# Splitting 520 tokens 240/280 instead of 260/260 in the dense products of a float32r macaron decoder layer

## The reference

```python
def half_ffn(x, g_pre, wg, wu, wd, g_post):
    return x + 0.5 * rmsnorm(swiglu(rmsnorm(x, g_pre), wg, wu, wd), g_post)
...
    hp = half_ffn(yp, *ffn1)
    fq, fk, fv, logf, nq, nkv, ng = project(rmsnorm(hp, g_mix_pre[l]), w_in[l], b_fox_f[l], pos_p)
    o_fox = fox_attention(fq, fk, fv, jnp.cumsum(logf, axis=1), pos_p)
    o_nsa = nsa_attention(nq, ng, nkv[:, :, :4], nkv[:, :, 4:], 0, pos_p, *cmp_w)
    hp = hp + rmsnorm(merge_groups(o_fox, o_nsa, g_fox_out[l], g_nsa_out[l], w_out[l]), g_mix_post[l])
    yp = half_ffn(hp, *ffn2)
```

## Time and profile before

| | |
|---|---|
| median of 3 runs | 1329.59 us (1329.27 to 1329.98) |
| span of the profiled execution | 1327.7 us; the median run is 1.9 us longer |
| PE busy / weight loads busy | 95% / 85% of the span |
| DVE, ACT, POOL busy | 43%, 34%, 13% |
| mean DMA rate | 89 GB/s |
| mean granted TensorE clock | 0.981 |

### The profile page before, as it was taken

The page is one execution under the profiler, slowest core; times in us unless marked ns, Lnnn a source line. Parts: engine busy times, 40 slices in busy tenths (PEclk is TensorE's granted clock), DMA queues, the critical chain, the costliest instruction groups (busy, mean ns, idle before and its releaser), DMA issues.

```text
span 1327.7 us, 22995 instructions
## 1 busy us (share of the span) xinstructions
PE 1259.9 (95%) x9234; PEld 1121.9 (85%) x9234; DVE 569.3 (43%) x896; ACT 454.3 (34%) x767; POOL 174.6 (13%) x157
## 2 busy tenths in 40 slices
PE   8999999999998898999999988798999999999994
PEld 6999999999996895499566543596999999999993
DVE  4334333343337665456533542636433333343333
ACT  5222212222335635442533432345322221222342
POOL 0111100101114001122101100034011100001113
PEclk9999999999999999999999989899999999999997
DMA  6222233222231241011600544011122222322221
GB/s 254 96 95 95 72 96 111 80 88 83 80 123 41 74 144 48 1 64 65 211 0 0 193 117 137 32 65 64 64 95 95 79 87 95 109 79 92 80 80 65
DMA packets 46001, 117.91 MB, mean 89 GB/s; under 512 B 4154, under 2 KB 21818, under 8 KB 39874
## 3 DMA queue, kind: packets, MB, share of 16 engines
q1 hardware_dynamic: 42738, 110.95, 24.8%
q10 hardware_dynamic: 3184, 5.88, 1.2%
HBM read 110.93 MB, written 7.97 MB: 90 GB/s over the span
## 4 chain that ended last, share of the span: by engine, by line
PE 87%; DVE 5%; ACT 3%; issue 2%; DMA 1%; POOL 1%; POOLq 0%; ACTq 0%; SPq 0%; DVEq 0%
PE ps L1308 68%; PE ps L1465 5%; PE ps L1479 3%; PE ps L1436 3%; PE ps L1451 2%; DVE UT L890 1%; PE ps L1317 1%; PE ps L1599 1%; DVE XL L870 1%; POOL H L1252 1%; DVE QST L964 1%; ACT QST L674 1%; PE ps L1608 1%; DMA RAW<-in_w_gu 0%; PE ps L1401 0%
## 5 line engine op out<-in xcount | busy, mean ns | idle before, releaser
L1308 PE MATMUL ps<-XH,WH 128*128 128x260 f32 x1904 | 390.6, 286 | 20.0 <-DVE XL L870 13.7
L1308 PE MATMUL ps<-XH,WL 128*128 128x260 f32 x1904 | 384.6, 284 | 0.0
L1308 PE MATMUL ps<-XL,WH 128*128 128x260 f32 x1904 | 384.2, 283 | 0.0
L403 ACT CAST WH<-RAW 128x1024 fp32r<-128x1024 f32 (+2 forms) x183 | 174.8, 956 | 505.1 <-PE ps L1308 495.8
L1308 PEld LDWEIGHTS ps<-XH,WH 128*128 128x128 f32 x1904 | 295.7, 189 | 27.6 <-DVE XL L870 14.0
L1308 PEld LDWEIGHTS ps<-XH,WL 128*128 128x128 f32 x1904 | 294.5, 189 | 0.0
L1308 PEld LDWEIGHTS ps<-XL,WH 128*128 128x128 f32 x1904 | 294.0, 189 | 0.0
L406 DVE TENSOR_TENSOR WL<-RAW,WH 128x1024 fp32r<-128x1024 f32 (+2 forms) x183 | 203.5, 1112 | 154.8 <-ACT WH L403 153.6
L1308 PE MATMUL ps<-UL,WH 128*128 128x260 f32 x704 | 141.9, 283 | 0.0
L1308 PE MATMUL ps<-UH,WL 128*128 128x260 f32 x704 | 141.5, 282 | 0.0
L1308 PE MATMUL ps<-UH,WH 128*128 128x260 f32 x704 | 141.4, 282 | 0.0
(11 more groups left out here) (229 smaller groups left out, 1056.5 us busy)
## 6 DMA issues: line engine op xcount, KB each, us to landing
RAW<-in_w_gu SPq DMA_DIRECT2D x44, 1024.0 KB, 4.8
RAW<-in_w_down SPq DMA_DIRECT2D x16, 768.0 KB, 4.6
RAW<-in_w_in SPq DMA_DIRECT2D x11, 1024.0 KB, 4.8
RAW<-in_w_down SPq DMA_DIRECT2D x16, 640.0 KB, 4.3
KF<-in_fox_k SPq DMA_DIRECT2D x16, 256.0 KB, 4.1
VF<-in_fox_v SPq DMA_DIRECT2D x16, 256.0 KB, 5.8
RAW<-in_w_out SPq DMA_DIRECT2D x4, 1024.0 KB, 5.0
H<-in_x SPq DMA_DIRECT2D x4, 520.0 KB, 7.4
```

Source lines behind the costliest of these rows:

```text
L403: nc.scalar.copy(WH[:, par, 0:width], RAW[:, slot, j, 0:width]).then_inc(w_hi, 1)
L1308: q = nc.tensor.matmul(ps[:, 2 * slot + half, 0:HALF], w[:, par, cols], x[:, kt0 + kt, half * HALF:(half + 1) * HALF], start=first and kt ...
```

## The change

`NA = 240` tokens are taken apart from the other 280. XH and XL become the two halves of one tile XX, UH and UL of one tile UU. Of a block, WH multiplies the high and the low part of the 240 tokens in one matmul of 480 columns; the two results lie side by side in one bank and are not added there. The 280 tokens go to the other bank with WH (high part), WH (low part) and WL, and WL·high of the 240 tokens is added onto the high result. The five matmuls have 480, 280, 280, 240 and 280 columns.

Whoever takes a tile out of PSUM must now add the low result to the high one. In `ffn` ACT first copies the low result (`lo_out`); DVE scales the 280 tokens, adds, and scales the 240 tokens (`scaled`). In `project` and for the output projection DVE does the copy as well.

```diff
@@ layer_kernel
+        def sums(slot):
+            a, b = 2 * slot, 2 * slot + 1
+            return ps[:, a, 0:NA], ps[:, a, NA:2 * NA], ps[:, b, 0:TOK - NA]
@@ scalar: ffn
                 def body(st):
+                    k = st.M * 2 + IT_F[f]
+                    if st.kind == "gu":
+                        act.wait_ge(used, k + 1)
+                        lo_out(GT[:, st.par, :], 0)
                     split_behind(f, st, 0)
...
+                        act.wait_ge(used, k + 2)
+                        lo_out(UT[:, st.par, :], 1)
+                    elif st.g == 0:
+                        act.wait_ge(used, k + 2)
+                        lo_out(row(Y, st.m), st.par)
                     split_behind(f, st, 1)
@@ vector
+            def scaled(dst, slot, f, n, downs):
+                a_hi, _, b = sums(slot)
+                nc.vector.tensor_tensor(dst[:, NA:TOK], b, R1[:, NA:TOK], ALU.mult)
+                dve.wait_ge(sem("lo_out"), since("lo_out", f, n + downs))
+                nc.vector.tensor_tensor(dst[:, 0:NA], dst[:, 0:NA], a_hi, ALU.add).then_inc(sem("joined"), 1)
+                dve.wait_ge(sem("joined"), since("joined", f, n))
+                return nc.vector.tensor_tensor(dst[:, 0:NA], dst[:, 0:NA], R1[:, 0:NA], ALU.mult)
@@ vector: ffn, down tiles of the second group
-                        nc.vector.tensor_tensor(two(row(Y, st.m)), two(row(Y, st.m)), halves(st.par),
-                                                ALU.add).then_inc(sem("evac"), 2)
+                        nc.vector.tensor_tensor(y[:, 0:NA], y[:, 0:NA], a_lo, ALU.add).then_inc(sem("joined"), 1)
+                        nc.vector.tensor_tensor(y[:, NA:TOK], y[:, NA:TOK], b, ALU.add)
+                        dve.wait_ge(sem("joined"), since("joined", f, st.m + (2 * FT + 1)))
+                        nc.vector.tensor_tensor(y[:, 0:NA], y[:, 0:NA], a_hi, ALU.add).then_inc(sem("evac"), 2)
@@ vector: project
-                        nc.vector.tensor_tensor(two(TR[:, j % 4, :]), halves(j % 2), two(R1[:, :]),
-                                                ALU.mult).then_inc(sem("projected"), 1)
+                        a_hi, a_lo, b = sums(j % 2)
+                        first = TR[:, j % 4, 0:NA]
+                        nc.vector.tensor_copy(first, a_lo).then_inc(sem("tr_lo"), 1)
+                        nc.vector.tensor_tensor(TR[:, j % 4, NA:TOK], b, R1[:, NA:TOK], ALU.mult)
+                        dve.wait_ge(sem("tr_lo"), j + 1)
+                        nc.vector.tensor_tensor(first, first, a_hi, ALU.add).then_inc(sem("tr_joined"), 1)
+                        dve.wait_ge(sem("tr_joined"), j + 1)
+                        nc.vector.tensor_tensor(first, first, R1[:, 0:NA], ALU.mult).then_inc(sem("projected"), 1)
@@ vector: output projection
-                nc.vector.tensor_copy(two(Y[:, t, :]), halves(t % 2)).then_inc(sem("ydone_b"), 1)
+                nc.vector.tensor_copy(Y[:, t, 0:NA], a_lo).then_inc(sem("y_lo"), 1)
+                nc.vector.tensor_copy(Y[:, t, NA:TOK], b)
+                dve.wait_ge(sem("y_lo"), t + 1)
+                nc.vector.tensor_tensor(Y[:, t, 0:NA], Y[:, t, 0:NA], a_hi, ALU.add).then_inc(sem("ydone_b"), 1)
@@ tensor: products
+                a_hi, _, b = sums(slot)
+                a_both = ps[:, 2 * slot, 0:2 * NA].rearrange("p (s n) -> p s n", s=2)
...
-                    for p, (w, x) in enumerate(((WH, xh), (WH, xl), (WL, xh))):
-                        for half in (0, 1):
-                            q = nc.tensor.matmul(ps[:, 2 * slot + half, 0:HALF], w[:, par, cols],
-                                                 x[:, kt0 + kt, half * HALF:(half + 1) * HALF],
+                    nc.tensor.matmul(a_both, hi, x[:, 0:2, k, 0:NA], start=start, stop=False, skip_group_check=True)
+                    nc.tensor.matmul(b, hi, x[:, 0, k, NA:TOK], start=start, stop=False)
+                    nc.tensor.matmul(b, hi, x[:, 1, k, NA:TOK], start=False, stop=False)
+                    nc.tensor.matmul(a_hi, lo, x[:, 0, k, 0:NA], start=False, stop=stop, skip_group_check=True)
+                    q = nc.tensor.matmul(b, lo, x[:, 0, k, NA:TOK], start=False, stop=stop)
```

More of the change, by code:

```diff
@@ L231, in layer_kernel @@
         xh0 = dense.at
-        XH = dense.put("XH", [P, KT, TOK], F32R)
-        xl0 = dense.at
-        XL = dense.put("XL", [P, KT, TOK], F32R)
+        XX = dense.put("XX", [P, 2, KT, TOK], F32R)
+        xl0 = xh0 + KT * tile_b
+        XH, XL = XX[:, 0], XX[:, 1]
         w_at = dense.at
@@ L629, in ffn, with lo_out @@
             def ffn(f, s):
+                def lo_out(dst, slot):
+                    nc.scalar.copy(dst[:, 0:NA], sums(slot)[1]).then_inc(sem("lo_out"), 1)
                 def body(st):
+                    k = st.M * 2 + IT_F[f]
+                    if st.kind == "gu":
+                        act.wait_ge(used, k + 1)
+                        lo_out(GT[:, st.par, :], 0)
                     split_behind(f, st, 0)
@@ L917, in body @@
                     dve.wait_ge(used, k + 2)
+                    a_hi, a_lo, b = sums(st.par)
+                    y = row(Y, st.m)
                     if st.g == 0:
-                        nc.vector.tensor_copy(two(row(Y, st.m)), halves(st.par)).then_inc(sem("evac"), 2)
-                    else:
-                        nc.vector.tensor_tensor(two(row(Y, st.m)), two(row(Y, st.m)), halves(st.par),
-                                                ALU.add).then_inc(sem("evac"), 2)
+                        nc.vector.tensor_copy(y[:, NA:TOK], b)
+                        dve.wait_ge(sem("lo_out"), since("lo_out", f, st.m + (2 * GROUPS[0] + 1)))
+                        nc.vector.tensor_tensor(y[:, 0:NA], y[:, 0:NA], a_hi, ALU.add).then_inc(sem("evac"), 2)
+                    else:
+                        nc.vector.tensor_tensor(y[:, 0:NA], y[:, 0:NA], a_lo, ALU.add).then_inc(sem("joined"), 1)
+                        nc.vector.tensor_tensor(y[:, NA:TOK], y[:, NA:TOK], b, ALU.add)
+                        dve.wait_ge(sem("joined"), since("joined", f, st.m + (2 * FT + 1)))
+                        nc.vector.tensor_tensor(y[:, 0:NA], y[:, 0:NA], a_hi, ALU.add).then_inc(sem("evac"), 2)
                     split_behind(f, st, 1)
@@ L1298, in ready, with products @@
                 pe.wait_ge(w_lo, k + 1)
-            def products(par, n, xh, xl, slot, first=True, last=True, kt0=0, arrived=None):
+            def products(par, n, x, slot, first=True, last=True, kt0=0, arrived=None):
+                a_hi, _, b = sums(slot)
+                a_both = ps[:, 2 * slot, 0:2 * NA].rearrange("p (s n) -> p s n", s=2)
                 for kt in range(n):
@@ L1304, in products @@
                         arrived(kt)
-                    cols = slice(kt * P, kt * P + P)
-                    for p, (w, x) in enumerate(((WH, xh), (WH, xl), (WL, xh))):
-                        for half in (0, 1):
-                            q = nc.tensor.matmul(ps[:, 2 * slot + half, 0:HALF], w[:, par, cols],
-                                                 x[:, kt0 + kt, half * HALF:(half + 1) * HALF],
-                                                 start=first and kt == 0 and p == 0,
-                                                 stop=last and kt == n - 1 and p == 2)
+                    hi, lo = (w[:, par, kt * P:kt * P + P] for w in (WH, WL))
+                    k = kt0 + kt
+                    start, stop = first and kt == 0, last and kt == n - 1
+                    nc.tensor.matmul(a_both, hi, x[:, 0:2, k, 0:NA], start=start, stop=False, skip_group_check=True)
[3 more added lines that the diff above has]
+                    q = nc.tensor.matmul(b, lo, x[:, 0, k, NA:TOK], start=False, stop=stop)
                 q.then_inc(used, 1)
@@ L1377, in body @@
                         ready(k + e)
-                        products((IT_F[f] + e) % 2, n, UH, UL, st.par, first=e == 0, last=e == 1, kt0=e * n,
+                        products((IT_F[f] + e) % 2, n, UU, st.par, first=e == 0, last=e == 1, kt0=e * n,
                                  arrived=arrived)
@@ L1630, in _ @@
                 arrived = (lambda kt: pe.wait_ge(sem("xlo"), since("xlo", "o", kt + 1))) if t == 0 else None
-                products((IT_OUT + t) % 2, KT, XH, XL, t % 2, arrived=arrived)
+                products((IT_OUT + t) % 2, KT, XX, t % 2, arrived=arrived)
             output_squares("b")
```

20 lines of the change are left out of this document (10 added, 10 removed).

## The result

The changed kernel takes **1337.29 us** (median of 4 runs, 1337.15 to 1338.98) against 1329.78 us of the kernel before on the same chip: a ratio of 1.0061, 95% interval 1.0047 to 1.0075. The forecast was 1332.9 and slower; it is slower, by 7.5 us where 3.3 were forecast.

A forecast was written before the change was run, and what follows sets the result against it. The prediction took PE's matmul pace as the bound, with DVE pacing PE in project. Terms of -5.7, +0.9 and +8.1 gave +3.3 us on 1329.6, so 1332.9 us, range 1324 to 1343.

The forecast's parts named there:

- Term 1: Dense products on PE: one matmul fewer per block saves 5 ns on each of 1144 blocks, 5.7 us less.
- Term 2: Taking tiles out of PSUM in feed-forwards and output projection: mostly hidden, only the ends pay, 0.9 us more.
- Term 3: Project: DVE's scaling takes 0.8 us more a tile in a chain without slack, so PE waits; 8.1 us more.
- The clock, taken at nothing: Longer PE waits may lower the clock; nothing in the sum, 3 us kept for the range.
- Narrow product: Rival: the 240-column float32r matmul runs at plain f32 pace, 0.40 us and not 0.11, near 1700 us; chance 0.14.
- Load pace: Rival: weight loads set the 0.120 us a matmul, 280 columns cost no more than 260; 1313 us, chance 0.05.
- Fixed excess: Rival: the whole 11.7 ns beside the columns goes with each matmul; 13.4 us less, 1325.2 us, chance 0.14.
- Waits that do not come: Rival: project's DVE chain has unseen slack; 1325 to 1329 us, held as part of the forecast's lower end.

The follow-up runs named there:

- the second trace: The changed kernel run once more, unaltered, for a second profile; 1337.73 us, ratio 1.0066 to the kernel before.
- project put back: The changed kernel with the input projection alone returned to six matmuls and one DVE scaling; 1326.49 us, ratio 0.9983 to the kernel before.
- UU moved as well: The kernel with project put back, with UU and all behind it 32 bytes further on; 1325.80 us, ratio 0.9975 to the kernel before.
- 256 in down: The kernel with project put back, with 256 tokens apart instead of 240 in the down products alone; 1325.06 us, ratio 0.9966 to the kernel before.
- project's four pieces: The kernel before, matmuls untouched, with DVE's scaling of a project tile in four dependent pieces; 1342.91 us, ratio 1.0103.

## Why the prediction was right, and where it was off

The sign and the mechanism were right: the products gain a little and project's chain on DVE loses more. The size was 3.3 us for 7.5. Step by step:

**Term 1 (-5.7): measured -4.0.** Over the blocks of XX at PE's pace, (688 + 56 + 48) x 5.0 = 4.0 us, which the feed-forwards bear out (1.7 and 1.6 us from first to last product start). The failed assumption is that one pace holds for every block: the 352 down blocks of two feed-forwards saved 0.5 ns (192 of them) or lost 0.7 (160), nothing in sum. And the 5 ns, exact in gate and up, were right for a wrong reason. I had derived them as the cost of one matmul; that cost is 9.1 ns there, and 4.1 are lost on the way to the new layout and its widths. The match of 5 with 5.0 is luck. The Trainium skill's page "TensorE: Matmul & The Clock Gate", section "Back-to-back issue gap", has 2.5 ns beside the columns, for an isolated warm matmul. The trace disagrees in gate and up, 5.0 and for the merge alone 9.1; the mean over all blocks, 4.0/1144 = 3.5, comes nearer to that than to my 5, but from numbers of both signs.

**Term 2 (+0.9): measured +0.6.** The ends of the first feed-forward, of the output projection and of the second feed-forward cost 0.17, 0.17 and 0.28 us, for 0.2, 0.35 and 0.35; the tiles inside are hidden, as said.

**Term 3 (+8.1): measured 8.3 for the same waits.** First stretch, from its second item on: PE is late by 0.6 us at items 4 and 5, 1.55 at item 6, 2.4 from item 7 on; forecast 0.8, 1.6, 2.5. Second stretch: 4.3 us ahead of the eighth tile and 4.2 at the end; forecast 4.0. The price of a tile was 0.94 and not 0.8, partly made good by PE's shorter blocks. I had put the wait ahead of one tile; it is spread over three. Ends: 0.83 us each for 0.8 (the second end is 1.35 in the first trace, where 1.2 GHz is granted from 639.2 on, and 0.83 in the second).

**The clock, taken at nothing, is the step that failed.** "I take nothing for it and keep 3 us for the range." The terms give -4.0 + 0.6 + 8.3 = +4.9; the two traces are 9.5 and 8.3 us longer (the medians 7.5 and 8.3). The rest is 3 to 5 us, in the stages where the lower clock was granted for longer: in the first trace 1.2 us in the first item of project, 0.5 in the first attention, 0.5 at the second end, 1.1 in the second attention and 1.0 behind it; in the second trace 0.6 in the first item, 1.4 at tile 7, 0.9 in the second attention and 0.3 behind it. The first item of project is one: its products wait for their operands four times in either kernel. Here are three pieces of it, 4 us each, before and changed (start and end; busy us of PE, PEld, DVE, ACT, POOL; granted clock; DMA share and rate):

```profile
409.00:413.00 4.00, 1.93 (x12) 1.55 (x12) 4.00 (x4) 1.74 (x4) 3.01 (x2) 1.00 0.00 0
413.00:417.00 4.00, 1.65 (x9) 1.45 (x10) 4.00 (x5) 2.19 (x4) 3.08 (x2) 0.87 0.00 0
417.00:421.00 4.00, 4.00 (x19) 3.43 (x18) 4.00 (x5) 2.43 (x4) 2.73 (x3) 0.70 0.00 0
```

```profile
409.00:413.00 4.00, 1.91 (x8) 1.50 (x9) 4.00 (x5) 2.08 (x4) 3.19 (x2) 0.69 0.00 0
413.00:417.00 4.00, 3.30 (x12) 2.72 (x12) 4.00 (x5) 2.51 (x4) 2.73 (x3) 0.50 0.01 2
417.00:421.00 4.00, 4.00 (x13) 3.37 (x12) 3.97 (x3) 1.81 (x3) 2.77 (x2) 0.53 0.00 0
```

The same waits, but 1.2 GHz is granted from 410.5 on instead of 415.9, and the item takes 17.16 us (16.58 in the second trace) for 15.94. With project put back it took 16.26, with UU moved as well 17.06, and with 256 in down 15.94, these three with the same code there: it varies with no cause in this stage that I can name. The first attention is another. Its window in the kernel before, the changed one, and with project put back:

```profile
507.00:556.00 49.00, 47.43 (x243) 25.51 (x244) 27.46 (x89) 26.45 (x81) 12.16 (x16) 0.97 0.00 1
```

```profile
507.00:556.00 49.00, 45.83 (x234) 25.45 (x234) 27.70 (x87) 25.90 (x78) 10.67 (x14) 0.93 0.02 6
```

```profile
507.00:556.00 49.00, 48.00 (x248) 25.35 (x252) 29.57 (x96) 26.98 (x83) 12.24 (x16) 1.00 0.00 1
```

With nothing at the lower clock the attention takes 46.42 us (the same in all four traces that have none), with 3.4 us of it 48.00 (47.7 to 48.0 in the six traces that have as much), with 5.9 48.50. The second attention takes 127.75 or 127.76 us in the four traces with none, and 128.30 to 128.91 in the eight with some; so what the attentions lose is the clock's. The changed kernel comes to them after a transpose that waited 2.4 us for v_new where it was 1.5.

That the change brings more of the lower clock is no chance of one trace. The mean granted clock was 0.973 to 0.976 in all eight runs of the changed kernel and 0.973 to 0.975 in the four of the kernel before with project's four pieces, where no matmul is changed; it was 0.977 to 0.981 in the 51 runs of the kernel before beside them, and 0.976 to 0.981 in the eleven with project put back. So the longer chain in project brings it. By which wait it does so stays open: the sums (51.5, 55.9, 66.7, 73.3 us) follow the waits, but single stretches don't.

**The rivals.** Narrow product: fallen, 240 columns take 0.11 us and 160 take 0.08. Load pace: fallen at these widths, since 280 columns take 0.127 us or more and not 0.120; a limit by the loads appears at 160. The Trainium skill's page "Perfetto Trace Analysis", section "Identifying the Most-Contended Engine", would read headroom from the 85% of the loads; the trace disagrees, since a sixth of the loads removed brought 0.7% of a block at best. Fixed excess of 11.7 ns: fallen as a forecast, 5.0 saved; as an account of one matmul's cost it was closer than mine in gate and up (9.1), and further off in the down products (3.9 and 2.0). Waits that do not come: fallen.

## What to carry to other kernels

Before merging matmuls, follow the results out of PSUM: here 5 ns a block were gained on PE and 0.94 us a tile lost where DVE is the pace setter, and the same change without that one stage is 0.2% faster (0.3% with widths fitted to each operand). A saving of a few ns a matmul can't be forecast from one pace for all: measure each kind of item, each width, and a small move of the operand. Where a change lengthens waits between matmuls, put a term in the sum for the stretches at the lower clock: here 15 to 22 us more of it cost 3 to 5 us, and a single stretch of 3.4 us cost 1.3 to 1.6 in the first attention and 0.5 to 1.0 in the second.

## What was unexpected in the hardware

- Moving the operand of the down products, and what stands behind it, by 32 bytes changed a block of five float32r matmuls from 720.7 to 716.7 ns.
- Six matmuls of 240 and 280 columns in the new layout take 724.9 ns where six of 260 take 720.8, with the same 1560 columns.
- A product that is shorter than the spacing of two weight loads (0.11 us) seems to delay not itself but the matmul behind it: 160 columns in 0.08 us, then 360 in 0.20 instead of 0.16. The rows show the delay; that the loads cause it was not tested by itself.
- Float32r shows no slow form at 240 or at 160 columns: 0.11 and 0.08 us to the next start.
- A longer chain on DVE between matmuls, with no matmul changed, went with a mean granted clock of 0.973 to 0.975 in every run, where it had been 0.977 to 0.981.
